# One of four token tiles leaves the dense expert products for gathered expert rows

## The reference

```
u = u_tab[i_blk]                                        # tokens x 128 rows of 1024
a = gelu(einsum('tkd,td->tk', u, h_blk))
out = einsum('tk,tkd->td', g_blk * a, v_tab[i_blk])
```

## Time and profile before

| | us |
|---|---|
| median of 3 runs (lowest to highest) | 4283.3 (4282.97 to 4284.61) |
| span of the profiled execution, the time the sums are made against | 4283.9 |
| TensorE busy in it | 4101.2 (96%) |
| VectorE, ScalarE, GpSimd busy | 2567.6 (60%), 1519.9 (35%), 2028.2 (47%) |
| DMA, mean over the span | 153 GB/s |

### The profile page before, as it was taken

One profiled execution on the slowest core, in us unless ns is written; L12 is line 12 of the kernel. 1 busy time (PEld: TensorE's weight loads), 2 busy tenths in 40 slices (PEclk: granted clock), 3 DMA queues, 4 the chain that ended last, 5 costly groups with the idle time before them and its releaser, 6 DMA issues. The chain is left out here.

```text
span 4283.9 us, 57205 instructions
## 1 busy us (share of the span) xinstructions
PE 4101.2 (96%) x18808; PEld 3356.0 (78%) x18808; DVE 2567.6 (60%) x4962; ACT 1519.9 (35%) x2716; POOL 2028.2 (47%) x1144
## 2 busy tenths in 40 slices
PE   7889999999999999999988899999999999999999
PEld 6467878888888788888873777778888887888887
DVE  7754416788677455555586534177886674555554
ACT  4263333433434322222233533333334343222222
POOL 4614343655656444444356052446556464444443
PEclk9999999999999999999999899999999999999999
DMA  4113134557575866666430231346574758666664
GB/s 136 36 52 104 62 104 148 180 168 210 156 211 157 258 196 191 191 195 191 132 106 28 67 99 52 103 162 191 161 214 150 208 164 255 190 192 195 190 193 137
DMA packets 505072, 657.31 MB, mean 153 GB/s; under 512 B 294144, under 2 KB 299648, under 8 KB 501376
## 3 DMA queue, kind: packets, MB, share of 16 engines
q1 hardware_dynamic: 203776, 520.12, 38.1%
q10 hardware_dynamic: 301056, 134.24, 11.3%
HBM read 508.49 MB, written 145.75 MB: 153 GB/s over the span
## 5 line engine op out<-in xcount | busy, mean ns | idle before, releaser
L1949 DVE TENSOR_TENSOR t_hots<-t_stages,t_hots 128x512 fp32r<-128x512 f32 x256 | 620.4, 2423 | 605.1 <-ACT t_hots L1763 605.0
L1802 POOL TENSOR_TENSOR t_ul<-t_u,t_uh 128x1024 fp32r<-128x1024 f32 x252 | 608.3, 2414 | 561.1 <-ACT t_uh L1701 561.1
L1974 PE MATMUL bank<-h_high,t_uh 128*128 128x512 f32 x2048 | 803.1, 392 | 15.0 <-ACTq L1771 12.9
L1974 PE MATMUL bank<-h_low,t_uh 128*128 128x512 f32 x2048 | 801.6, 391 | 0.0
L1974 PE MATMUL bank<-h_high,t_ul 128*128 128x512 f32 x2048 | 798.3, 390 | 0.0
L2016 PE MATMUL bank<-t_v_early,t_hots 128*128 128x512 f32 x3072 | 712.3, 391 | 12.5 <-DVE t_hots L1949 12.5
L2016 PE MATMUL bank<-h_high,t_hots 128*128 128x512 f32 x3072 | 706.7, 389 | 0.0
L2016 PEld LDWEIGHTS bank<-t_v_early,t_hots 128*128 128x128 f32 x3072 | 580.4, 189 | 134.3 <-DVE t_hots L1949 13.3
L2016 PEld LDWEIGHTS bank<-h_high,t_hots 128*128 128x128 f32 x3072 | 576.7, 188 | 119.6
L1819 POOL TENSOR_TENSOR t_v_early<-t_stages,t_v_early 128x1024 fp32r<-128x1024 f32 x128 | 306.4, 2394 | 393.8 <-ACT t_v_early L1759 393.8
L1819 POOL TENSOR_TENSOR h_high<-t_stages,h_high 128x1024 fp32r<-128x1024 f32 x128 | 307.7, 2405 | 380.4 <-ACT h_high L1759 380.4
(11 more groups left out here) (394 smaller groups left out, 6058.0 us busy)
## 6 DMA issues: line engine op xcount, KB each, us to landing
t_u<-in_peer_u SPq DMA_DIRECT2D x256, 512.0 KB, 3.6
t_stages<-in_peer_v SPq DMA_DIRECT2D x256, 512.0 KB, 4.1
acts<-t_act ACTq DMA_DIRECT2D x256, 256.0 KB, 3.0
gates<-t_stages ACTq DMA_DIRECT2D x128, 512.0 KB, 5.3
t_stages<-acts SPq DMA_DIRECT2D x256, 256.0 KB, 4.2
t_stages<-gates SPq DMA_DIRECT2D x256, 256.0 KB, 4.4
p_w_raw<-in_peer_wq SPq DMA_DIRECT2D x64, 256.0 KB, 3.1
m_w_raw<-in_w_in SPq DMA_DIRECT2D x48, 256.0 KB, 2.6
```

The lines of the kernel that those rows point to most:

```text
L1802: e.tensor_tensor(ul[:, n % 2, :, :], u[:, n % 2, :, :], uh[:, n % 2, :, :].bitcast(F32), ALU.subtract).then_inc(u_split, 1)
L1949: e.tensor_tensor(al[:, s, :], a_in[:, s, :], ah[:, s, :].bitcast(F32), ALU.subtract).then_inc(act_split, 1)
L1974: mm = e.matmul(k.bank[n % 2][:, :], a[:, n % 2, q, :], b[:, q, :], start=(q == 0 and m == 0), stop=(q == KT - 1 and m == 2))
```

## The change

Token tile 0 leaves the dense way. Its 128 x 128 pairs of token and expert are **gathered**: for each of a token's 128 picks j, one indirect DMA from GpSimd's queue fetches 128 rows of u (one for each token, 512 KB), and VectorE takes the dot product with h of the tile, which lies in PSUM (`dot`); in the value stage the same with rows of v, weighted and added into a sum in PSUM (`add_value`). The dense products, activations and gates cover 384 tokens, in 128 chunks without tile stretches: tile 0 is routed first, tiles 1, 2 and 3 are spread in 16 chunks each from chunk 34, 69 and 104. The dots stand in VectorE's program between the steps of routes 1 to 3 (18 each) and behind jobs (24, 24, 26). The one-hot rows are plain fp32 now, so that a job is 4 matmuls of 128 columns and one eviction of 512, with no low part on GpSimd or VectorE. u has three buffers, and ScalarE and GpSimd may be three chunks ahead. In the value stage VectorE takes the low part of v, GpSimd issues gathers, and TensorE does 6 blocks x 3 matmuls in a chunk.

```diff
@@ peer_scores, scalar @@
+                e.wait_ge(scalar_freed, 32)
+                e.activation(k.pair[3][:, :], xn[:, 0, :], ACT.Copy).then_inc(h_kept, 1)
@@ peer_experts, sync @@
+                def load_u(n):
+                    if n >= 2 + U_SLOTS:
+                        e.wait_ge(u_split, n - U_SLOTS - 1)
+                    e.dma_start(u[:, n % U_SLOTS, :, :], ut[n]).then_inc(u_loaded[n % U_SLOTS], 16)
@@ scalar @@
+                def gelu(n):
+                    e.wait_ge(a_done, n + 1)
...
+                    if n + U_SLOTS < NKEY:
+                        round_u(n + U_SLOTS)
                     if n >= 1:
+                        store_act(n - 1)
...
+                def evict(t, q):
...
+                    e.wait_ge(g_done, job(t, q) + 1)
+                    at = SET * q % HALF
+                    e.activation(stage[half][:, :, at:at + SET], g_bank(job(t, q)).rearrange("p (t n) -> p n t", t=SET),
+                                 ACT.Copy).then_inc(staged, 1)
...
+                for n in range(NKEY):
...
+                    gelu(n)
...
+                        for q in range(JOBS):
+                            if START[t] + (STEPS * (q + 1) - 1) // KT == n:
+                                evict(t, q)
+                                if q >= JOBS // 2 and q % 2 == 1:
+                                    store_gates(t, 0, (q - JOBS // 2) // 2)
+                        piece = n - START[t] - JOBS * STEPS // KT
+                        if 0 <= piece < PIECES:
+                            store_gates(t, 1, piece)
@@ gpsimd @@
+                def gather_row(j):
+
+                    if j >= R_SLOTS:
+                        e.wait_ge(dotted, j - R_SLOTS + 1)
+                    e.indirect_dma_start(row_slot[j % R_SLOTS], None, u_rows,
+                                         bass.IndirectOffsetOnAxis(ap=idx[:, j:j + 1], axis=0)).then_inc(row_got[j % R_SLOTS], 16)
...
+                for n in range(2, NKEY):
+                    split_u(n)
+                    for j in range(KK):
+                        if gather_after(j) == n:
+                            if j == 0:
+                                e.wait_ge(idx_ready, 1)
+                            gather_row(j)
+                e.wait_ge(stored[1], 16 * (PIECES - 1) * (TT - 1))
+                e.wait_ge(stored_first[1], 16 * (TT - 1))
+                for n in range(2, NKEY):
+                    for j in ((2 * n - 4, 2 * n - 3) if n < 6 else (n + 2,)):
+                        if j < KK:
+                            gather_value(j)
@@ vector @@
+                def dot(some=1):
+
+                    for _ in range(some):
+                        j = rows_done.n
+                        slot = row_slot[j % R_SLOTS]
+                        e.wait_ge(row_got[j % R_SLOTS], 16 * (j // R_SLOTS + 1))
+                        e.tensor_tensor_reduce(out=slot, in0=slot, in1=h_own, scale=1.0, scalar=0.0, op0=ALU.mult, op1=ALU.add,
+                                               accum_out=dots[:, j:j + 1]).then_inc(dotted, rows_done.one())
...
+                def split_value(n):
+
+                    e.wait_ge(v_round, n + 1)
+                    e.tensor_tensor(vl[n % RING], v[:, n % RING, :], vh[n % RING].bitcast(F32), ALU.subtract).then_inc(v_split, 1)
+
+                def add_value(n):
+                    slot, w = value_slot[n % V_SLOTS], weights[:, n:n + 1]
+                    e.wait_ge(value_got[n % V_SLOTS], 16 * (n // V_SLOTS + 1))
...
+                        e.wait_ge(added, n)
+                        e.scalar_tensor_tensor(out=own_sum, in0=slot, scalar=w, in1=own_sum, op0=ALU.mult, op1=ALU.add).then_inc(added, 1)
...
+                for n in range(NKEY):
+                    if n + 1 < NKEY:
+                        gate(n + 1)
+                    low(n)
+                    split_value(n)
+                    add_value(n)
@@ tensor @@
+                    out = k.bank[n % 2][:, 0:DENSE].rearrange("p (t n) -> p t n", n=P)
...
+                            mm = e.matmul(out, a[n % U_SLOTS][:, q, :], b[:, 1:TT, q, :],
                                           start=(q == 0 and m == 0), stop=(q == KT - 1 and m == 2))
...
+                def spread(t, q):
+
+                    n = job(t, q)
+                    if n >= 2:
+                        e.wait_ge(staged, n - 1)
+                    e.wait_ge(oh_ready, 2 * n + 2)
+                    for a in range(SET):
+                        mm = e.matmul(g_bank(n)[:, a * NKEY:(a + 1) * NKEY], first[:, q % 2, a, :], second[:, q % 2, a, :], start=True, stop=True)
+                    mm.then_inc(g_done, 1)
```

More of the change, by code:

```diff
@@ L1594, in peer_experts @@
         sel = sb("sel", [P, 3, KK])
[L1595 to L1600, removed]
+        base = sb("base", [P, 1])
+        idx, own_gate, dots, weights = sb("idx", [P, KK], U32), sb("own_gate", [P, KK]), sb("dots", [P, KK]), sb("weights", [P, KK])
@@ L1605, in peer_experts @@
         half_v = RING * DM
         v = stages[:, 0, 0:half_v].rearrange("p (r d) -> p r d", r=RING)
-        a_in, g_in = (stages[:, 0, half_v + n * RING * SEQ:half_v + (n + 1) * RING * SEQ].rearrange("p (r t) -> p r t", r=RING)
+        a_in, g_in = (stages[:, 0, half_v + n * RING * SEQ:half_v + (n + 1) * RING * SEQ].rearrange("p (r t) -> p r t", r=RING)[:, :, 0:DENSE]
                       for n in range(2))
-        ah, al = (hots[:, 2 * n:2 * n + 2, :].rearrange("p x (r t) -> p (x r) t", t=SEQ) for n in range(2))
+        with ExitStack() as until_values:
+            rows = k.sb("t_rows", [P, 6, DM], F32, ctx=until_values)
+            first, second = (k.sb("t_" + n, [P, 2, SET, NKEY], F32, ctx=until_values) for n in ("first", "second"))
@@ L1641, in load_scores @@
                 def load_scores(t):
[L1642 to L1657, removed]
-                            load_value(0, n - CHUNKS + 2 + RING)
+                    sem, _ = scores_landed(t)
+                    e.dma_start(scores_at(t), scores[t]).then_inc(sem, 16)
+                def load_u(n):
+                    if n >= 2 + U_SLOTS:
+                        e.wait_ge(u_split, n - U_SLOTS - 1)
+                    e.dma_start(u[:, n % U_SLOTS, :, :], ut[n]).then_inc(u_loaded[n % U_SLOTS], 16)
                 def load_value(turn, n):
@@ L1747, in tile @@
-                    for n in range(CHUNKS - tail, CHUNKS):
-                        gelu(t, n, last)
-                        own = PIECES if last else PIECES - LATER
-                        for piece in range(own):
-                            if piece * tail // own == n - CHUNKS + tail:
-                                store_gates(t, 1, piece)
-                        if last and n >= CHUNKS - 2:
-                            round_value(0, n - CHUNKS + 2)
-                    store_act(t, CHUNKS - 1)
@@ L1934, in _, with gate @@
+                        dot(due_in_jobs(t, q))
                 e.tensor_copy(iota_p, k.iota[:, 0:TOPK]).then_inc(ramp_ready, 1)
                 e.wait_ge(ramp_ready, 1)
-                with e.Fori(0, TT - 1) as t:
-                    tile(t)
-                tile(TT - 1)
-                def gate(turn, n):
+                route(0)
+                for t in range(1, TT):
+                    route(t)
+                    spread(t)
+                assert rows_done.n == KK
+                def gate(n):
@@ new lines, in _ @@
+                for n in range(NKEY):
+                    busy = [t for t in range(1, TT) if 0 <= n - START[t] < JOBS * STEPS // KT]
+                    for t in range(1, TT):
+                        if n == START[t] - 1:
+                            e.wait_ge(sel_ready, t + 1)
+                            for a in range(3):
+                                e.transpose(k.bank[2][:, a * P:(a + 1) * P], sel[:, a, :], k.ident[:, :]).then_inc(turned, 1)
+                    if not busy:
+                        experts(n, 0, KT)
+                    for t in busy:
+                        for part in range(KT // STEPS):
+                            spread(t, (n - START[t]) * (KT // STEPS) + part)
+                            experts(n, part * STEPS, (part + 1) * STEPS)
@@ L2008, in chunk @@
+                def chunk(turn, n, begins, ends):
                     s = n % RING
```

414 lines of the change are left out of this document (210 added, 204 removed).

## The result

After the change the kernel takes 4054.9 us (median of 4 runs, 4047.9 to 4064.9) where before it took 4284.0 (4283.0 to 4287.1): a ratio of 0.9465, 95% interval 0.945 to 0.948. It is faster, and 4054.9 lies at the very top of the range (3740 to 4060). The gain is 229 us where 436 were forecast. In the profiled execution (span 4063.1) it is 221.

A forecast was written before the change was run, and what follows sets the result against it. TensorE was taken to bound both long stages. Dense stage 712 us for 765 (53 less) and value stage 165 less, times 2 layers, make 436: 4284 - 436 = 3848 us, range 3740 to 4060.

The forecast's parts named there:

- eviction wait: Spreads of the dense stage: TensorE waits for ScalarE's eviction, now behind gelu and rounding; 2.2 us, 15 times a spread.
- dense stage outside the spreads, a layer: Dense stage without its three spreads: 351 us, plus 3.4 for the lower clock and 16 for store windows.
- value stage, a layer: Value stage: 768 of 3072 matmuls go, 18 left in a chunk of 4.05 us; 165 us less a layer.
- 74 in 8.43 us, 0.114 each: Spreads: new fp32 gate products priced from the fp32 key products, 0.114 us each; 44 us for 60.
- with one period at the lower clock: Dense stage: the clock falls once, after the 15 us wait for route 1; +3.4 us.
- Route 1: Dense stage: route with 18 dots ends at 153 us; TensorE reaches chunk 33 at 138 and waits 15.
- The store windows: Dense stage: 24 chunks with extra stores take 4.85 us instead of 4.18, bound by DMA at 365 GB/s; +16 us.
- 1 (the eviction costs nothing): Spreads: VectorE bounds them, 90 for 114 us, some 70 us less a layer; 3710 us; chance 7%.
- 2 (DMA bounds the value stage): Value stage: at 296 GB/s a chunk takes 4.87 us, +105 a layer; 4060 us; chance 8%.
- 3 (passes of 2.09): VectorE's passes take 2.09 us: longer routes, value chunks of 4.3 us; 3975 us; chance 8%.
- 4 (the issue holds VectorE): Value stage: GpSimd's gather issue holds VectorE's passes, 4.55 us a chunk, +64 a layer; 3975 us; chance 10%.
- 5 (issue of 4.4 us or more): Both stages: GpSimd's gather issues are the bound, slower than before; 4500 us at 4.8 us each; chance 6%.

The follow-up runs named there:

- e1: The changed kernel with both evictions of a chunk put back ahead of its gelu in ScalarE's program; 3734.0 us.
- e4: The changed kernel with gate products in fp32r instead of fp32, leaving out the part of each gate below fp32r; 3895.6 us.
- e2: The changed kernel with the eviction wait kept but filled by seven TensorE products of the identity that nobody reads; 3937.2 us.
- e3: The changed kernel with one part undone: GpSimd takes the low part of v again in the value stage; 4089.3 us.
- e5: Against e1: the first six rows gathered one chunk sooner, all others two chunks later; 4127.6 us.
- e7: Against e1: the 128 gathers and dot products of the dense stage left out; 3668.0 us.

## Why the prediction was right or wrong

The direction, the ways in which the time is spent, and the value stage were right; the size was wrong by half, in one place, 48 chunks of a layer. Per chunk of a spread 7.29 us were forecast and 9.38 measured. Over both layers:

| step of the prediction | forecast | measured | us |
|---|---|---|---|
| gate products of a job | 4 x 0.114 = 0.46 | 0.89 (e1, e4) | 0.43 x 192 = 83 |
| clock in the spreads | no fall | 70 falls at 1.6 (9.8 - 8.2; e2) | 112 |
| eviction wait | 2.2 | 2.29 (e1) | 0.09 x 90 = 8 |
| dense stage outside the spreads, a layer | 351 + 3.4 + 16 = 370 | 373, 377 | 10 |
| value stage, a layer | 540 | 538.3, 541.3 | 0 |

Together 213 of the 215 us that the profiled execution lacks; what is left is within what runs differ by ahead of the change's stages (the dense stage of layer 1 begins anywhere from 672.3 to 676.6 us in the runs here).

**First failed step: "74 in 8.43 us, 0.114 each".** An fp32 product leaves two records, so 74 records are 37 products of 0.228 us. The trace of before said so. One line's own view, and ScalarE's timeline beside the key products, where each eviction takes the result of four:

```profile
L1549 PE MATMUL bank<-p_keys,p_qT x256: 270/275/275, 651.4 to 2795.4; 128*128 128x128 f32 x128
```

```profile
655.19 0.60 ACT L1513 ACTIVATE p_s<-bank 128x512 f32<-128x512 f32 x1 [0.30 <-PE bank L1549]
656.08 0.60 ACT L1513 ACTIVATE p_s<-bank 128x512 f32<-128x512 f32 x1 [0.30 <-PE bank L1549]
```

256 records for 4 tiles x 16 keys x 2 layers = 128 products, and 0.89 us for four of them. The Trainium skill, FP8 and Floating Point Precision, § TensorE Precision Notes, says that true fp32 takes four passes through the array. The trace agrees: four times 128 columns are 512, which take 0.225 us in the earlier trace rows, and a product took 0.223.

**Second failed step: "with one period at the lower clock".** The forecast charged a fall of the clock to the one long wait alone and took the 15 short ones of a spread at their own length. The earlier trace rows showed a fall behind 5.8 us of idle, and no shorter gap was read. The trace of before has falls behind shorter ones. One, at the start of the cross attention, in TensorE's timeline:

```profile
403.13 0.47 PE L314 MATMUL bank<-x_w_high,x_hh 128*128 128x512 f32 x1 [1.91 <-DVE x_hl L232]
...
404.10 0.63 PE L314 MATMUL bank<-x_w_high,x_hh 128*128 128x512 f32 x1
404.53 0.63 PE L314 MATMUL bank<-x_w_low,x_hh 128*128 128x512 f32 x1
...
407.31 0.40 PE L314 MATMUL bank<-x_w_high,x_hl 128*128 128x512 f32 x1
407.54 0.40 PE L314 MATMUL bank<-x_w_high,x_hh 128*128 128x512 f32 x1
```

Behind 1.91 us of idle the starts are 0.43 us apart, later 0.23 again. The same stands behind 1.83 us at 2532.77, and nothing of it behind 1.66 us at 3187.51. So the risk could be read from the trace of before; that it would come behind 70 of 90 gaps could not. e2 shows that it is the gap, not the products.

**What held.** The order of ScalarE's program made the wait, at the place and of the length worked out from the earlier trace rows; the step said that all later expert matmuls stand behind it. VectorE has slack in the spreads (e1: 63.5 busy of 70). Route 1 made TensorE wait: 5.2 us and 6.7 for two splits of u standing behind gathers, 12 for the 15 forecast. The store windows, forecast at 16 us, cost 12.0 and 17.6 us of waits for gelu. The size is met, but not by chunks that last as long as their bytes: ScalarE stands at its own DMA issue, and the gelu behind it is late. ScalarE's timeline in one such window; TensorE waits 3.82 us for this gelu:

```profile
1258.37 7.32 ACTq L1752 DMA_DIRECT2D acts<-t_act  x1
...
1266.47 0.49 ACT L1758 ACTIVATE t_act<-pair 128x384 f32<-128x384 f32 x1 [6.78 <-issue]
```

VectorE's value chunk fits TensorE's. That the value stage meets 540 to within 2 us is in part luck: the second value chunk starts at 17.4 us instead of 14.5, and the 3 us set aside for DMA were not needed in its middle, where a matmul takes 0.227 us as before.

**The rivals.** 1 (the eviction costs nothing): no, but e1 is the kernel it describes, 3734 for its 3710, with TensorE (70.00 of 70) and not VectorE as the bound of the spreads. 2 (DMA bounds the value stage): no, 222 matmuls in 50 us, though at a DMA share of 1.00. 3 (passes of 2.09): no, 1.21 and 1.28. 4 (the issue holds VectorE): no, 553 and 557 ns beside issues; GpSimd's own passes do hold it (e3). 5 (issue of 4.4 us or more): no, 1.02. The range held the result, but not by the case that set its upper end.

## What to carry to other kernels

Price a new wait of TensorE by what it does to the clock, not by its length alone: 2 us of waiting at each chunk cost 2.3 + 1.2 here (the wait, and 112 us of falls over 90 waits), and moving one call in another engine's program gave back more than the whole change had gained. Before dividing a stretch by its records, check the count against the code. And when prefetches are moved, look at the stage where the buffers cover least.

## What was not expected of the hardware

Falls behind the same 2.01 us gap went from 70 to 29 of 90 when the work between gaps was 5.1 us (7.35 - 2.29) instead of 5.95; no fall came with the gap at 0.45 us (e2). The number is not fixed for one program: e3, with the same spreads, had 63.

A DMA issue on ScalarE takes 0.34 us at the median. After the change 47 of 352 took over 1 us (18 of 384 before), up to 7.4, and in e5 one took 10.6: behind each of the first two spreads and near the end of the dense stage, where gate pieces and activations are stored beside the loads. The gelu behind such an issue was late with it. e7 bears on the cause: without gathered rows ScalarE's program is the same, the DMA share between spreads falls from 1.05 to 0.85, and no issue there passes 1.4 us, where e1 has up to 7.9. The load of the DMA engines is thus the likely cause; it was not varied by itself.

In one stretch of 50 us (1550 to 1600, after the change) the DMA engines moved 393 GB/s at a share of 1.03, more than the 365 that the prediction took for the densest.
